# Two transformer layers behind an expert block on one Trainium2 core: the attention's last projection as seven block products

## The chip, the cores and the metric

The kernel runs on one core of one Trainium2 chip. The metric is the device time of one execution in microseconds (us), as the median of several runs. The engines are named by their work: TensorE multiplies matrices (PE in the profile, PEld for its weight loads), VectorE is DVE, ScalarE is ACT, GpSimd is POOL, and SyncE (SP) issues the transfers. Everything is in 32-bit floats.

## The reference, cut to what matters

There are 256 tokens of 1024 features. A first block (a hybrid mixer and 32 routed experts) is followed by two equal layers. Only the end of a layer's attention part is touched:

```python
for l in range(DEPTH_2):                       # 2 layers
    ...                                        # two attentions give y_a, y_b (256 x 512)
    merged = gate_a * (y_a @ w_proj_a[l]) + gate_b * (y_b @ w_proj_b[l])   # 256 x 1024
    x = x + merged @ w_out[l]                  # w_out 1024 x 1024: the product changed here
    h = rms_norm_2(x, norm_ffn[l])
    u = causal_dwconv(h @ w_up[l], conv_w[l], conv_b[l])
    val, gat = u[..., :D_FF], u[..., D_FF:]
    x = x + (jax.nn.silu(gat) * val) @ w_down[l]
```

## The kernel before, in words

The five engines run five written-out programs, and semaphores are all that ties them. Each engine takes its instructions in the order in which they were written. There is no planner; the order of work is the order of the text, in `layers_t` (TensorE), `layers_v` (VectorE), `layers_s` (ScalarE), `layers_pool` (GpSimd) and `layers_sync` (SyncE).

**Tiles.** Tokens lie in two tiles of 128 (`tt`), features in eight tiles of 128 (`KT` = 8), and output columns in two halves of 512 (`CH`). One accumulator bank holds 128 x 512 floats; the eight banks are dealt out in turn by `layer_plan`. TensorE waits for `room` in a bank, fills it and raises `full`; the engine that empties it raises `free`, on which `taken` and the next `room` wait. A 32-bit product of one 128 x 128 tile with 128 x 512 appears in the trace as two MATMUL records.

**Weights.** In the layers a ring of four slots (2 MB each) holds the weights. SyncE loads load n into slot n mod 4 as soon as the last reader of load n-4 has raised its flag; `loads2` lists each load with its reader. The two halves of `w_out` are loads 14 and 15, in slots 2 and 3.

**The stretch around the change, by engine.** TensorE: the last values product (L2358), then the second gated projection `pb` in four banks (`project_t`, L2407), then the output projection `wo` (L2416 to L2424): for each token tile and each column half, eight products over the features, 32 in all. Then twelve short bfloat16 products that nobody reads (`keep_running`, L597), and the transposes of the normed `h`, first token tile 0, then tile 1 (`features_by_tile`, L2282); then the up projection (L606).

VectorE: the four banks of the first projection `pa` times their gates (L2056); for each of four `pb` banks a product with the gates (L2060) and the sum of both (L2064), which writes two feature tiles of `mT` and raises `mg`; then `norm_v`: each bank of `wo` is added to its quarter of x as it comes (L1878), and for each token tile ScalarE squares both quarters (L2131), VectorE sums (L1884), GpSimd takes the root (L1823) and VectorE scales x into `h` (L1894). Tile 0 is normed while TensorE still works on tile 1.

**The down projection is already made the other way.** Its inner dimension is taken in 11 pairs of feature tiles. For a pair the left factor is a 2 x 2 block matrix (token tiles by the two feature tiles: a11, a12, a21, a22), and the right factor too (the two feature tiles by column halves: b11 to b22). Seven products replace eight:

```
s1 = a21 + a22   s2 = s1 - a11   s3 = a11 - a21   s4 = a12 - s2
t1 = b12 - b11   t2 = b22 - t1   t3 = b22 - b12   t4 = b21 - t2
dm0 = a11 b11    dn0 = a12 b21   dn1 = s4 b22     dn3 = s1 t1
dm1 = s2 t2      dm2 = s3 t3     dn2 = a22 t4
u = dm0 + dm1    quarter 0 = dm0 + dn0            quarter 1 = u + dn3 + dn1
quarter 2 = u + dm2 + dn2                         quarter 3 = u + dm2 + dn3
```

`act_sums` (L2072 to L2075, four operations of 128 x 128) and `weight_sums` (L2084 to L2087, four of 128 x 512) make the sums on VectorE; `top_sums` and `low_sums` in `norm_v` put the seven banks together (L1843 to L1867). A helper `then(ins)` makes VectorE wait for its own instruction where the next reads what it wrote.

Of the kernel before, what the change touches and what calls it, by code (L numbers as in the profile page):

```python
# [18 lines left out]
ALU = mybir.AluOpType  # L19
# [92 lines left out]
def layer_plan():  # L112
    p = Plan()
    for name, n in (("hT", 4), ("cv", 1), ("qi", 2), ("m1", 2), ("m2", 2), ("kiT", 1), ("ix0", 2), ("ix1", 4),
# [4 lines left out]
                    ("wo", 4), ("fT", 4), ("up", 2 * UPC), ("dm", 3), ("dn", 4)):  # L119
        p.add(name, n)  # L120
    return p
# [109 lines left out]
def split(ap, n):  # L231
    return ap.rearrange("p (a b) -> p a b", a=n)
# [47 lines left out]
    "yconv", "fexp", "act",  # L280
    "a_sum", "w_sum", "pair",
    "out",
# [3 lines left out]
def build_program(nc, A, consts, out):  # L286
# [4 lines left out]
    with ctx:  # L291
# [45 lines left out]
        def area(at, n):  # L337
            return arena[:, at:at + n]
# [1378 lines left out]
        loads2.append((4, D, [cols("w_proj_a_2", 0, D)], ("pa", 3)))  # L1717
        loads2.append((4, D, [cols("w_proj_b_2", 0, D)], ("pb", 3)))
        for i in range(2):
            loads2.append((KT, CH, [cols("w_out_2", i * CH, (i + 1) * CH)], ("wo", 2 + i)))  # L1720
        for i in range(UPC):
# [54 lines left out]
        def layers_sync(sp):  # L1776

            sp.wait_ge(S["acc_f"], 1)
            for l in range(LAYERS):
                BL = layer_banks(l)  # L1780
                for n, (kts, width, srcs, reader) in enumerate(loads2):
# [16 lines left out]
                    if n == RING2 - 1:  # L1798
# [5 lines left out]
                        sp.dma_start(normw[0][:], A["norm_ffn_2"][l].partition_broadcast(P)).then_inc(L["in_ffn"], 16)  # L1804
                    if reader == ("wo", 3):

                        if l < LAYERS - 1:
                            layer_params(sp, l + 1)
# [28 lines left out]

        def norm_v(v, BL, name, event, w, then=None):

            def quarter(j):  # L1840
                return x[:, j // 2, j % 2 * CH:(j % 2 + 1) * CH]

            def top_sums():  # L1843
                u, y = yval[0], yval[1]
                v.wait_ge(*BL.ready("dm", 0))
                then(v.tensor_tensor(quarter(0), quarter(0), BL.bank("dm", 0)[:], ALU.add))
                v.wait_ge(*BL.ready("dm", 1))
                v.tensor_copy(u, BL.bank("dm", 0)[:]).then_inc(BL.free("dm", 0), 1)
                v.wait_ge(*BL.taken("dm", 0))
                v.tensor_tensor(u, u, BL.bank("dm", 1)[:], ALU.add).then_inc(BL.free("dm", 1), 1)  # L1850
                v.wait_ge(*BL.ready("dn", 0))
                v.tensor_tensor(quarter(0), quarter(0), BL.bank("dn", 0)[:], ALU.add).then_inc(BL.free("dn", 0), 1)
                v.wait_ge(*BL.ready("dn", 3))
                v.wait_ge(*BL.taken("dm", 1))
                then(v.tensor_tensor(y, u, BL.bank("dn", 3)[:], ALU.add))
                then(v.tensor_tensor(quarter(1), quarter(1), y, ALU.add))
                v.wait_ge(*BL.ready("dn", 1))
                v.tensor_tensor(quarter(1), quarter(1), BL.bank("dn", 1)[:], ALU.add).then_inc(BL.free("dn", 1), 1)

            def low_sums():  # L1860
                u = yval[0]
                then(v.tensor_tensor(quarter(3), quarter(3), BL.bank("dn", 3)[:], ALU.add))
                v.wait_ge(*BL.ready("dm", 2))
                v.tensor_tensor(u, u, BL.bank("dm", 2)[:], ALU.add).then_inc(BL.free("dm", 2), 1)
                v.wait_ge(*BL.taken("dm", 2))
                then(v.tensor_tensor(quarter(2), quarter(2), u, ALU.add))
                v.tensor_tensor(quarter(3), quarter(3), u, ALU.add).then_inc(BL.free("dn", 3), 1)  # L1867

            for tt in range(TT):
                if name == "dn" and tt == 0:  # L1870
                    top_sums()
                elif name == "dn":
                    v.wait_ge(*BL.ready("dn", 2))
                    v.tensor_tensor(quarter(2), quarter(2), BL.bank("dn", 2)[:], ALU.add).then_inc(BL.free("dn", 2), 1)
                else:
                    for j in (2 * tt, 2 * tt + 1):
                        v.wait_ge(*BL.ready(name, j))
                        v.tensor_tensor(quarter(j), quarter(j), BL.bank(name, j)[:], ALU.add).then_inc(BL.free(name, j), 1)  # L1878
                if event == 2 * LAYERS:
# [4 lines left out]
                v.tensor_scalar(ms[:, tt:tt + 1], sa[:, tt, 0:1], sa[:, tt, 1:2], EPS, ALU.add, ALU.add).then_inc(L["ms"], 1)  # L1884
                if name == "dn" and tt == 0:
                    low_sums()
# [11 lines left out]

        V_LINKS = 109 + 2 * UPC + 2 * UPC + 5

        def layers_v(v):
            for l in range(LAYERS):
# [150 lines left out]
                for j in range(4):  # L2053
                    g = gate_s[:, 2 * j:2 * j + 2, :]
                    v.wait_ge(*BL.ready("pa", j))
                    v.tensor_tensor(g, split(BL.bank("pa", j)[:], 2), g, ALU.mult).then_inc(BL.free("pa", j), 1)  # L2056
                for j in range(4):
                    t = split(mtmp[j % 2], 2)
                    v.wait_ge(*BL.ready("pb", j))
# [7 lines left out]
                def act_sums(p):  # L2067
                    s1, s2, s3, s4 = (a_sums[p][:, i, :] for i in range(4))
                    a11, a21 = (actT[:, 2 * p, tt * P:(tt + 1) * P] for tt in range(TT))
                    a12, a22 = (actT[:, 2 * p + 1, tt * P:(tt + 1) * P] for tt in range(TT))  # L2070
                    v.wait_ge(L["act"], UPC * l + p + 1)
                    then(v.tensor_tensor(s1, a21, a22, ALU.add))  # L2072
                    v.tensor_tensor(s3, a11, a21, ALU.subtract)
                    then(v.tensor_tensor(s2, s1, a11, ALU.subtract))
                    v.tensor_tensor(s4, a12, s2, ALU.subtract).then_inc(L["a_sum"], 1)  # L2075

                def weight_sums(p):
                    t1, t2, t3, t4 = (w_sums[p % HELD][:, i, :] for i in range(4))
                    w, landed, value = w2_slot(NL - DNC + p // 2, l)
                    k = 2 * p % 4  # L2080
                    b11, b12 = w[:, k, 0:CH], w[:, k, CH:D]
                    b21, b22 = w[:, k + 1, 0:CH], w[:, k + 1, CH:D]
                    v.wait_ge(landed, value)
                    then(v.tensor_tensor(t1, b12, b11, ALU.subtract))  # L2084
                    v.tensor_tensor(t3, b22, b12, ALU.subtract)
                    then(v.tensor_tensor(t2, b22, t1, ALU.subtract))
                    v.tensor_tensor(t4, b21, t2, ALU.subtract).then_inc(L["w_sum"], 1)  # L2087

# [160 lines left out]
        def layers_t(pe):  # L2249
            for l in range(LAYERS):  # L2250
# [618 lines left out]
```

## Time and profile before

| | |
|---|---|
| median of 3 runs | 2212.95 us (2206.88 to 2217.66) |
| profiled execution, its own time | 2206.54 us |
| its span in the trace | 2204.5 us |
| granted TensorE clock, mean | 0.993 |
| TensorE busy | 2115.7 us, 96% |
| VectorE busy | 979.7 us, 44% |
| output projection in layer 0 | 1479.7 to 1507.2 us |
| output projection in layer 1 | 1948.5 to 1976.0 us |

The span is the stretch from the first to the last instruction; the execution's own time is 2.04 us longer. In the rows a "bank" is an accumulator, "ring" the weight slots and everything that lies in the two idle ones, "arena", "hbuf" and "hTbuf" are working areas. Idle time in brackets stands ahead of the instruction, with what ended it. The clock that TensorE was granted (PEclk) is given as a share of full speed: 1.00 is 2.4 GHz and 0.50 is 1.2 GHz.

### The profile page before, as it was taken

To read this page: it belongs to the slowest core of one execution; us is meant where nothing else is said; L and a number is where in the kernel's file an instruction comes from. 1 tells how busy PE (TensorE), PEld (TensorE's weight loads), DVE (VectorE), ACT (ScalarE), POOL (GpSimd) and SP (SyncE) were. 2 spreads that over 40 slices of the span, in tenths; PEclk is the share of its full clock that TensorE was granted. 3 is DMA by queue.
4 is the path that set the end of the run, shared out by engine and by line. 5 is a ranking of instruction groups with operands and counts; after the bars stand their busy time and mean duration, and the time that the engine had idled before them with its cause. 6 is when DMAs were issued, how large, how long until landed. Compare 5 with 4: busy or idle time off the path is not lost.

```text
span 2204.5 us, 24055 instructions
## 1 busy us (share of the span) xinstructions
PE 2115.7 (96%) x9704; PEld 1164.4 (53%) x9704; DVE 979.7 (44%) x1561; ACT 333.7 (15%) x737; POOL 48.3 (2%) x30
## 2 busy tenths in 40 slices
PE   6998999999999999999999899999999999999999
PEld 4855743333333333333333365886885557868874
DVE  1555535333323333223332226843676256725684
ACT  1123110000000000000000112321110113311110
POOL 0000200000000000000000002000000011000000
PEclk9988999999999999999999999999999999999999
DMA  9556079999998999999999754343443534243441
GB/s 371 209 222 266 18 249 402 428 428 429 428 425 325 428 429 428 428 428 429 428 429 428 284 192 172 115 135 124 151 151 129 179 117 168 100 153 120 153 162 63
DMA packets 132001, 590.91 MB, mean 268 GB/s; under 512 B 9142, under 2 KB 65638, under 8 KB 104026
## 3 DMA queue, kind: packets, MB, share of 16 engines
q1 hardware_dynamic: 131930, 589.90, 67.6%
q8 instruction: 53, 0.87, 0.2%
q14 instruction: 18, 0.15, 0.0%
HBM read 588.81 MB, written 3.16 MB: 269 GB/s over the span
## 4 chain that ended last, share of the span: by engine, by line
PE 70%; DMA 21%; DVE 5%; ACT 2%; issue 1%; POOL 1%; SPq 0%; POOLq 0%; DVEq 0%
PE bank L606 21%; DMA ring<-in_w_dram 20%; PE bank L1415 18%; PE bank L616 8%; PE bank L2444 6%; PE bank L2407 3%; PE bank L819 2%; PE bank L2422 2%; PE bank L1469 1%; PE bank L1396 1%; PE bank L2787 1%; DMA ring<-in_w_ada_dram 1%; PE bank L543 1%; PE bank L1428 1%; PE bank L2358 1%
## 5 line engine op out<-in xcount | busy, mean ns | idle before, releaser
L1415 PE MATMUL bank<-ring,arena 128*64 128x512 f32 x3168 | 702.7, 595 | 28.3 <-DMA ring<-in_w_dram 27.6
L606 PE MATMUL bank<-hTbuf,ring 128*128 128x256 f32 x2368 | 515.9, 380 | 2.8 <-ACT hTbuf L2676 2.6
L606 PEld LDWEIGHTS bank<-hTbuf,ring 128*128 128x128 f32 x2368 | 450.1, 190 | 67.1 <-issue 5.9
L1415 PEld LDWEIGHTS bank<-ring,arena 128*64 128x64 f32 x3168 | 219.6, 137 | 500.5 <-issue 428.8
L1117 DVE TENSOR_SCALAR arena<-bank 128x512 f32<-128x512 f32 x33 | 22.8, 692 | 395.9 <-PE bank L1415 395.9
L616 PE MATMUL bank<-ring,hTbuf 128*128 128x512 f32 (+2 forms) x384 | 151.2, 554 | 0.0
L2097 DVE SCALAR_TENSOR_TENSOR arena<-bank,arena 128x254 f32<-128x254 f32 (+1 forms) x176 | 76.6, 477 | 84.4 <-ACT arena L2241 82.8
L616 PEld LDWEIGHTS bank<-ring,hTbuf 128*128 128x128 f32 x384 | 72.6, 190 | 75.1 <-issue 71.8
L1121 DVE RECIPROCAL arena<-arena 128x512 f32<-128x512 f32 x33 | 110.6, 3353 | 1.1
L1242 ACT ACTIVATE arena<-arena 128x512 f32<-128x512 f32 x33 | 20.8, 629 | 535.0 <-DVE arena L1117 535.0
L1141 DVE TENSOR_TENSOR arena<-bank,arena 128x512 f32<-128x512 f32 x33 | 22.8, 692 | 128.4 <-PE bank L1415 128.4
L2241 ACT ACTIVATE arena<-bank,arena 128x256 f32<-128x256 f32 x88 | 44.9, 561 | 209.4 <-PE bank L606 209.4
L2109 DVE RECIPROCAL arena<-arena 128x512 f32<-128x512 f32 x22 | 73.8, 3353 | 0.8
L1469 PE MATMUL bank<-arena 64*128 64x512 f32 x264 | 65.6, 615 | 8.0 <-DVE arena L1141 8.0
L1396 PE MATMUL bank<-hbuf,arena 128*64 128x512 f32 x256 | 62.0, 605 | 0.0
L2407 PE MATMUL bank<-arena,ring 128*128 128x256 f32 (+1 forms) x320 | 56.8, 339 | 0.0
L2422 PE MATMUL bank<-ring 128*128 128x512 f32 x128 | 55.3, 592 | 0.0
L1238 ACT ACTIVATE arena<-bank 128x512 f32<-128x512 f32 x33 | 19.7, 597 | 228.4 <-PE bank L1403 228.4
L2407 PEld LDWEIGHTS bank<-arena,ring 128*128 128x128 f32 x320 | 50.4, 191 | 5.4 <-issue 0.7
L2023 DVE RECIPROCAL arena<-arena 128x1024 f32<-128x1024 f32 x8 | 52.4, 6553 | 0.3
L1137 DVE COPY arena<-bank 128x256 f32<-128x256 f32 x33 | 14.0, 424 | 73.6 <-PE bank L1409 73.6
L2444 PE MATMUL bank<-arena 128*128 128x512 f32 x96 | 44.1, 592 | 0.0
(462 smaller groups left out, 1849.0 us busy)
## 6 DMA issues: line engine op xcount, KB each, us to landing
ring<-in_w_dram SPq DMA_DIRECT2D x192, 2048.0 KB, 22.6
ring<-in_w_up_dram SPq DMA_DIRECT2D x44, 1024.0 KB, 7.0
ring<-in_w_in_dram SPq DMA_DIRECT2D x21, 2048.0 KB, 8.6
ring<-in_w_ada_dram SPq DMA_DIRECT2D x12, 2048.0 KB, 8.6
ring<-in_w_down_dram SPq DMA_DIRECT2D x10, 2048.0 KB, 7.8
ring<-in_w_out_dram SPq DMA_DIRECT2D x6, 2048.0 KB, 8.0
ring<-in_w_in_dram SPq DMA_DIRECT2D x4, 1024.0 KB, 13.8
ring<-in_w_proj_a_dram SPq DMA_DIRECT2D x2, 2048.0 KB, 8.3
```

Source lines behind the costliest of these rows:

```text
L606: ins = pe.matmul(B.bank(name, j)[:, i * T:(i + 1) * T], w[:, k, (first + i) * P:(first + i + 1) * P], hT[:, k, :], start=(k == 0), stop=( ...
L616: ins = pe.matmul(B.bank(name, j)[:, 0:width], xs(k), ws(k), start=(k == 0), stop=(k == kts - 1))
L1121: v.reciprocal(eb, eb).then_inc(F["s1"], 1)
L1396: ins = pe.matmul(XB[g * SLOTS:(g + 1) * SLOTS, :], psel[:, tt, :], h[:, tt, g * CH:(g + 1) * CH], start=(tt == 0), stop=(tt == 1))
L1415: ins = pe.matmul(bank[g * SLOTS:(g + 1) * SLOTS, :], lhsT, rhs[:, g * CH:(g + 1) * CH], start=start, stop=stop)
L1469: pe.matmul(ACC[2 * tt + g][:], pgt[par][64 * g:64 * g + 64, tt, :], ysb[64 * g:64 * g + 64, :], start=False, stop=False, skip_group_check ...
L2023: v.reciprocal(gs, gs).then_inc(L["gsig"], 1)
L2097: ins = v.scalar_tensor_tensor(out=y2[:, k, back:], in0=pb[:, k, 0:T - back], scalar=conv_cols[:, 44 * (2 - back) + m:44 * (2 - back) + m ...
L2109: then(v.reciprocal(fe[i % 2], fe[i % 2]))
L2407: ins = pe.matmul(BL.bank(name, j)[:, i * T + c0:i * T + c1], w[:, k, (2 * j + i) * P:(2 * j + i + 1) * P], src[:, k, c0:c1], start=(k == ...
L2422: ins = pe.matmul(BL.bank("wo", 2 * tt + half)[:], mT[:, k, tt * P:(tt + 1) * P], ws[half][:, k, :], start=(k == 0), stop=(k == KT - 1))
L2444: return pe.matmul(bank[:], lhsT, rhs, start=(p == 0), stop=(p == NPR - 1))
```

## The change

The output projection is made by the same seven products, with four pairs of feature tiles (p = 0 to 3). Three more banks (`wm`) are dealt out ahead of `wo`, which moves all later banks by three. VectorE makes the sums of the weights (`out_sums`: waits until both halves of `w_out` have landed, then four operations of 128 x 512) and of the gated sums (`mix_sum`, four of 128 x 128). Pairs 0 and 1 of `out_sums` stand ahead of the loop over the `pb` banks, pairs 2 and 3 inside it, ahead of the evacuation of bank 2 and of bank 3. `norm_v` now treats `wo` as it treated `dn`. Both halves of `w_out` name `wm` bank 1 as the reader that frees their slots. The four helpers `left_sums`, `right_sums`, `act_sums` and `weight_sums` do what the old text of the last two did.

```diff
-                    ("wo", 4), ("fT", 4), ("up", 2 * UPC), ("dm", 3), ("dn", 4)):
+                    ("wm", 3), ("wo", 4), ("fT", 4), ("up", 2 * UPC), ("dm", 3), ("dn", 4)):
...
+        mix_sums = [split(area(at, 4 * P), 4) for at in (6 * D, 6 * D + 4 * P, 8 * D, 8 * D + 4 * P)]
+        wo_sums = [split(buf, 4) for buf in (area(4 * D, 4 * CH), hTbuf[:], extra(2 * D, 4 * CH), area(11776, 4 * CH))]
...
-            loads2.append((KT, CH, [cols("w_out_2", i * CH, (i + 1) * CH)], ("wo", 2 + i)))
+            loads2.append((KT, CH, [cols("w_out_2", i * CH, (i + 1) * CH)], ("wm", 1)))
...
+            more = {"dn": "dm", "wo": "wm"}.get(name)
...
             for tt in range(TT):
-                if name == "dn" and tt == 0:
+                if tt == 0:
                     top_sums()
-                elif name == "dn":
-                    v.wait_ge(*BL.ready("dn", 2))
-                    v.tensor_tensor(quarter(2), quarter(2), BL.bank("dn", 2)[:], ALU.add).then_inc(BL.free("dn", 2), 1)
                 else:
-                    for j in (2 * tt, 2 * tt + 1):
-                        v.wait_ge(*BL.ready(name, j))
-                        v.tensor_tensor(quarter(j), quarter(j), BL.bank(name, j)[:], ALU.add).then_inc(BL.free(name, j), 1)
+                    v.wait_ge(*BL.ready(name, 2))
+                    v.tensor_tensor(quarter(2), quarter(2), BL.bank(name, 2)[:], ALU.add).then_inc(BL.free(name, 2), 1)
...
+                def mix_sum(p):
+                    v.wait_ge(L["mg"], 4 * l + p + 1)
+                    left_sums(mT, p, mix_sums[p], L["mix_sum"])
+
+                def out_sums(p):
+                    halves = [w2_slot(N_WO + half, l) for half in range(2)]
+                    for w, landed, value in halves:
+                        v.wait_ge(landed, value)
+                    (b11, b12), (b21, b22) = ([w[:, 2 * p + k, :] for w, landed, value in halves] for k in range(2))
+                    right_sums(b11, b12, b21, b22, wo_sums[p], L["wo_sum"])
+
+                out_sums(0)
+                out_sums(1)
                 for j in range(4):
+                    if j >= 2:
+                        out_sums(j)
                     t = split(mtmp[j % 2], 2)
                     v.wait_ge(*BL.ready("pb", j))
...
                     v.tensor_tensor(mT[:, 2 * j:2 * j + 2, :], gate_s[:, 2 * j:2 * j + 2, :], t, ALU.add).then_inc(L["mg"], 1)
-                norm_v(v, BL, "wo", 2 * l + 1, normw[0])
+                    mix_sum(j)
+                norm_v(v, BL, "wo", 2 * l + 1, normw[0], then)
...
-                for tt in range(TT):
-                    for half in range(2):
-                        pe.wait_ge(*BL.room("wo", 2 * tt + half))
-                        for k in range(KT):
-                            if tt == 0 and half == 0 and k % 2 == 0:
-                                pe.wait_ge(L["mg"], 4 * l + k // 2 + 1)
-                            ins = pe.matmul(BL.bank("wo", 2 * tt + half)[:], mT[:, k, tt * P:(tt + 1) * P], ws[half][:, k, :],
-                                            start=(k == 0), stop=(k == KT - 1))
-                        ins.then_inc(BL.full("wo", 2 * tt + half), 1)
+                for name, n in (("wm", 3), ("wo", 4)):
+                    for j in range(n):
+                        pe.wait_ge(*BL.room(name, j))
+
+                def out_product(name, j, lhs, rhs):
+                    for p in range(4):
+                        ins = pe.matmul(BL.bank(name, j)[:], lhs(p), rhs(p), start=(p == 0), stop=(p == 3))
+                    ins.then_inc(BL.full(name, j), 1)
+
+                for p in range(4):
+                    pe.wait_ge(L["mg"], 4 * l + p + 1)
+                    ins = pe.matmul(BL.bank("wm", 0)[:], mT[:, 2 * p, 0:P], ws[0][:, 2 * p, :], start=(p == 0), stop=(p == 3))
+                ins.then_inc(BL.full("wm", 0), 1)
+                out_product("wo", 0, lambda p: mT[:, 2 * p + 1, 0:P], lambda p: ws[0][:, 2 * p + 1, :])
+                pe.wait_ge(L["mix_sum"], 4 * l + 4)
+                out_product("wo", 1, lambda p: mix_sums[p][:, 3, :], lambda p: ws[1][:, 2 * p + 1, :])
+                pe.wait_ge(L["wo_sum"], 4 * l + 4)
+                out_product("wo", 3, lambda p: mix_sums[p][:, 0, :], lambda p: wo_sums[p][:, 0, :])
+                out_product("wm", 1, lambda p: mix_sums[p][:, 1, :], lambda p: wo_sums[p][:, 1, :])
+                out_product("wm", 2, lambda p: mix_sums[p][:, 2, :], lambda p: wo_sums[p][:, 2, :])
+                out_product("wo", 2, lambda p: mT[:, 2 * p + 1, P:T], lambda p: wo_sums[p][:, 3, :])
```

## Rows read from the trace of the kernel before

**Rows 1.** The page's table of engines: busy time, share of the span, instructions.
```profile
PE 2115.7 (96%) x9704; PEld 1164.4 (53%) x9704; DVE 979.7 (44%) x1561; ACT 333.7 (15%) x737; POOL 48.3 (2%) x30
```
**Rows 2.** The page's chain of waits that ended last, by engine.
```profile
PE 70%; DMA 21%; DVE 5%; ACT 2%; issue 1%; POOL 1%; SPq 0%; POOLq 0%; DVEq 0%
```
**Rows 3.** TensorE's timeline, layer 0: start, duration, engine, line, operation, count, idle before.
```profile
1465.65 14.20 PE L2407 MATMUL bank<-arena,ring 128*128 128x128 f32 x80
...
1479.69 27.63 PE L2422 MATMUL bank<-ring 128*128 128x512 f32 x64
1507.16 2.75 PE L597 MATMUL bank<-con 128*128 128x512 bf16 x12
1509.75 1.04 PE L2282 MATMUL bank<-con,hbuf 128*128 128x128 f32 x8
1511.19 1.09 PE L2282 MATMUL bank<-con,hbuf 128*128 128x128 f32 x8 [0.40 <-DVE hbuf L1894]
```
**Rows 4.** VectorE's timeline of the same stretch.
```profile
1461.70 0.69 DVE L2056 TENSOR_TENSOR arena<-bank,arena 128x512 f32<-128x512 f32 x1 [2.02 <-PE bank L2407]
1469.53 0.69 DVE L2060 TENSOR_TENSOR arena<-bank,arena 128x512 f32<-128x512 f32 x1 [7.14 <-PE bank L2407]
1470.25 0.69 DVE L2064 TENSOR_TENSOR ring<-arena 128x512 f32<-128x512 f32 x1
1472.98 0.69 DVE L2060 TENSOR_TENSOR arena<-bank,arena 128x512 f32<-128x512 f32 x1 [2.04 <-PE bank L2407]
...
1480.62 0.69 DVE L2064 TENSOR_TENSOR ring<-arena 128x512 f32<-128x512 f32 x1
...
1507.36 0.69 DVE L1878 TENSOR_TENSOR x<-x,bank 128x512 f32<-128x512 f32 x1 [6.18 <-PE bank L2422]
```
**Rows 5.** VectorE's timeline in layer 0's down projection: its sums.
```profile
1673.43 0.29 DVE L2072 TENSOR_TENSOR arena<-ring 128x128 f32<-128x128 f32 x1
...
1674.50 0.68 DVE L2084 TENSOR_TENSOR hTbuf<-ring 128x512 f32<-128x512 f32 x1
...
1677.15 0.68 DVE L2084 TENSOR_TENSOR arena<-ring 128x512 f32<-128x512 f32 x1
```
**Rows 6.** SyncE's timeline: the issue of both halves of w_out in layer 0.
```profile
1418.07 19.16 SPq L1796 DMA_DIRECT2D ring<-in_w_out_dram  x2
```
**Rows 7.** The page's DMA issues: count, KB each, median us to landing.
```profile
ring<-in_w_out_dram SPq DMA_DIRECT2D x6, 2048.0 KB, 8.0
```
**Rows 8.** VectorE's timeline behind layer 0's down projection (norm_v with dn).
```profile
1719.03 0.69 DVE L1848 COPY arena<-bank 128x512 f32<-128x512 f32 x1 [1.88 <-PE bank L2444]
...
1726.76 0.69 DVE L1858 TENSOR_TENSOR x<-x,bank 128x512 f32<-128x512 f32 x1 [1.23 <-PE bank L2444]
...
1728.36 0.68 DVE L1862 TENSOR_TENSOR x<-x,bank 128x512 f32<-128x512 f32 x1
...
1730.78 0.69 DVE L1867 TENSOR_TENSOR x<-x,arena 128x512 f32<-128x512 f32 x1
1731.39 1.41 DVE L1894 SCALAR_TENSOR_TENSOR hbuf<-x,small,normw 128x512 f32<-128x512 f32 x2
1732.71 0.68 DVE L1874 TENSOR_TENSOR x<-x,bank 128x512 f32<-128x512 f32 x1
```
**Rows 9.** TensorE's timeline behind layer 0's down projection.
```profile
1731.63 2.75 PE L597 MATMUL bank<-con 128*128 128x512 bf16 x12
...
1737.13 1.09 PE L2282 MATMUL bank<-con,hbuf 128*128 128x128 f32 x8 [1.87 <-DVE hbuf L1894]
```
**Rows 10.** TensorE's timeline in the first block: two of its idle stretches.
```profile
34.84 7.44 PE L606 MATMUL bank<-hTbuf,ring 128*128 128x256 f32 x26 [2.58 <-ACT hTbuf L2676]
...
210.33 2.05 PE L819 MATMUL bank<-hbuf,arena 128*128 128x128 f32 x16 [3.21 <-DVE arena L717]
```
**Rows 11.** Stretches of 1 us: busy time of each engine, granted clock, DMA share, GB/s.
```profile
35.00:36.00 1.00, 1.00 (x3) 0.82 (x4) 0.00 (x0) 0.00 (x0) 0.00 (x0) 0.50 1.01 424
...
211.00:212.00 1.00, 1.00 (x12) 1.00 (x10) 0.00 (x0) 0.47 (x1) 0.00 (x0) 1.00 1.15 492
```

More of the change, by code:

```diff
@@ L280 @@
     "yconv", "fexp", "act",
-    "a_sum", "w_sum", "pair",
+    "a_sum", "w_sum", "pair", "mix_sum", "wo_sum",
     "out",
@@ L1718, in build_program @@
         loads2.append((4, D, [cols("w_proj_b_2", 0, D)], ("pb", 3)))
+        N_WO = len(loads2)
         for i in range(2):
-            loads2.append((KT, CH, [cols("w_out_2", i * CH, (i + 1) * CH)], ("wo", 2 + i)))
+            loads2.append((KT, CH, [cols("w_out_2", i * CH, (i + 1) * CH)], ("wm", 1)))
         for i in range(UPC):
@@ L1804, in layers_sync @@
                         sp.dma_start(normw[0][:], A["norm_ffn_2"][l].partition_broadcast(P)).then_inc(L["in_ffn"], 16)
-                    if reader == ("wo", 3):
+                    if n == N_WO + 1:
                         if l < LAYERS - 1:
@@ L1836, in layers_pool, with norm_v @@
                 roots_p(pool, 2 * l + 1)
-        def norm_v(v, BL, name, event, w, then=None):
+        def norm_v(v, BL, name, event, w, then):
             def quarter(j):
                 return x[:, j // 2, j % 2 * CH:(j % 2 + 1) * CH]
+            more = {"dn": "dm", "wo": "wm"}.get(name)
             def top_sums():
                 u, y = yval[0], yval[1]
[L1845 to L1855, printed above, removed]
+                v.wait_ge(*BL.ready(more, 0))
+                then(v.tensor_tensor(quarter(0), quarter(0), BL.bank(more, 0)[:], ALU.add))
+                v.wait_ge(*BL.ready(more, 1))
+                v.tensor_copy(u, BL.bank(more, 0)[:]).then_inc(BL.free(more, 0), 1)
+                v.wait_ge(*BL.taken(more, 0))
+                v.tensor_tensor(u, u, BL.bank(more, 1)[:], ALU.add).then_inc(BL.free(more, 1), 1)
+                v.wait_ge(*BL.ready(name, 0))
+                v.tensor_tensor(quarter(0), quarter(0), BL.bank(name, 0)[:], ALU.add).then_inc(BL.free(name, 0), 1)
+                v.wait_ge(*BL.ready(name, 3))
+                v.wait_ge(*BL.taken(more, 1))
+                then(v.tensor_tensor(y, u, BL.bank(name, 3)[:], ALU.add))
@@ L1856, in top_sums @@
                 then(v.tensor_tensor(quarter(1), quarter(1), y, ALU.add))
-                v.wait_ge(*BL.ready("dn", 1))
-                v.tensor_tensor(quarter(1), quarter(1), BL.bank("dn", 1)[:], ALU.add).then_inc(BL.free("dn", 1), 1)
+                v.wait_ge(*BL.ready(name, 1))
+                v.tensor_tensor(quarter(1), quarter(1), BL.bank(name, 1)[:], ALU.add).then_inc(BL.free(name, 1), 1)
             def low_sums():
                 u = yval[0]
-                then(v.tensor_tensor(quarter(3), quarter(3), BL.bank("dn", 3)[:], ALU.add))
@@ L1863, in low_sums @@
-                v.wait_ge(*BL.ready("dm", 2))
-                v.tensor_tensor(u, u, BL.bank("dm", 2)[:], ALU.add).then_inc(BL.free("dm", 2), 1)
-                v.wait_ge(*BL.taken("dm", 2))
+                then(v.tensor_tensor(quarter(3), quarter(3), BL.bank(name, 3)[:], ALU.add))
+                v.wait_ge(*BL.ready(more, 2))
+                v.tensor_tensor(u, u, BL.bank(more, 2)[:], ALU.add).then_inc(BL.free(more, 2), 1)
+                v.wait_ge(*BL.taken(more, 2))
                 then(v.tensor_tensor(quarter(2), quarter(2), u, ALU.add))
-                v.tensor_tensor(quarter(3), quarter(3), u, ALU.add).then_inc(BL.free("dn", 3), 1)
+                v.tensor_tensor(quarter(3), quarter(3), u, ALU.add).then_inc(BL.free(name, 3), 1)
@@ L1884, in norm_v @@
                 v.tensor_scalar(ms[:, tt:tt + 1], sa[:, tt, 0:1], sa[:, tt, 1:2], EPS, ALU.add, ALU.add).then_inc(L["ms"], 1)
-                if name == "dn" and tt == 0:
+                if tt == 0:
                     low_sums()
@@ L1897, in norm_v @@
                 ins.then_inc(L["h_new"], 1)
-        V_LINKS = 109 + 2 * UPC + 2 * UPC + 5
+        V_LINKS = 109 + 4 * UPC + 16 + 10
         def layers_v(v):
@@ L2056, in layers_v, with left_sums, right_sums, act_sums @@
                     v.tensor_tensor(g, split(BL.bank("pa", j)[:], 2), g, ALU.mult).then_inc(BL.free("pa", j), 1)
+                def left_sums(src, p, out, flag):
+                    s1, s2, s3, s4 = (out[:, i, :] for i in range(4))
+                    a11, a21 = (src[:, 2 * p, tt * P:(tt + 1) * P] for tt in range(TT))
+                    a12, a22 = (src[:, 2 * p + 1, tt * P:(tt + 1) * P] for tt in range(TT))
+                    then(v.tensor_tensor(s1, a21, a22, ALU.add))
+                    v.tensor_tensor(s3, a11, a21, ALU.subtract)
+                    then(v.tensor_tensor(s2, s1, a11, ALU.subtract))
+                    v.tensor_tensor(s4, a12, s2, ALU.subtract).then_inc(flag, 1)
+                def right_sums(b11, b12, b21, b22, out, flag):
+                    t1, t2, t3, t4 = (out[:, i, :] for i in range(4))
+                    then(v.tensor_tensor(t1, b12, b11, ALU.subtract))
+                    v.tensor_tensor(t3, b22, b12, ALU.subtract)
+                    then(v.tensor_tensor(t2, b22, t1, ALU.subtract))
+                    v.tensor_tensor(t4, b21, t2, ALU.subtract).then_inc(flag, 1)
+                def act_sums(p):
+                    v.wait_ge(L["act"], UPC * l + p + 1)
+                    left_sums(actT, p, a_sums[p], L["a_sum"])
+                def weight_sums(p):
+                    w, landed, value = w2_slot(NL - DNC + p // 2, l)
+                    k = 2 * p % 4
+                    v.wait_ge(landed, value)
+                    right_sums(w[:, k, 0:CH], w[:, k, CH:D], w[:, k + 1, 0:CH], w[:, k + 1, CH:D], w_sums[p % HELD], L["w_sum"])
+                def mix_sum(p):
[4 more added lines that the diff above has]
+                    for w, landed, value in halves:
+                        v.wait_ge(landed, value)
+                    (b11, b12), (b21, b22) = ([w[:, 2 * p + k, :] for w, landed, value in halves] for k in range(2))
+                    right_sums(b11, b12, b21, b22, wo_sums[p], L["wo_sum"])
+                out_sums(0)
+                out_sums(1)
                 for j in range(4):
+                    if j >= 2:
+                        out_sums(j)
                     t = split(mtmp[j % 2], 2)
@@ L2064, in layers_v @@
                     v.tensor_tensor(mT[:, 2 * j:2 * j + 2, :], gate_s[:, 2 * j:2 * j + 2, :], t, ALU.add).then_inc(L["mg"], 1)
-                norm_v(v, BL, "wo", 2 * l + 1, normw[0])
[L2067 to L2087, printed above, removed]
+                    mix_sum(j)
+                norm_v(v, BL, "wo", 2 * l + 1, normw[0], then)
                 for i in range(UPC):
```

## The prediction

> **What bounds the kernel now.** I read the table of engines first: TensorE is busy for 96% of the span and VectorE for 44% [rows 1]. Then the chain of waits: TensorE holds 70% of it and transfers 21% [rows 2]; by its lines the transfers belong to the expert weights of the first block, far from this change. So inside the layers the order of TensorE's work is the time, and the timelines of one stretch decide. TensorE goes from the second gated projection (ends 1479.69) into the output projection without a gap, and out of it at 1507.16 into the filler products [rows 3]. Behind it stands a tail that no product hides: the last bank is added at 1507.36, and the transposes of token tile 1 start at 1511.19 [rows 3, 4], 4.03 us after the last product. Layer 1 shows the same distances. VectorE, meanwhile, waits: 7.14 us before bank 0 of the second projection and about 2 us before each later one [rows 4]. These gaps are where the new sums have to fit.
>
> **The change part by part.** I call E the moment at which TensorE starts the fillers, 1507.16 before.
>
> *Four products fewer.* 64 records take 27.47 us (1507.16 - 1479.69), so one of the 32 products takes 0.858 us. Four fewer save 3.43 us a layer. All of it is on the path.
>
> *Sums on VectorE.* A set of four 128 x 512 sums takes 2.65 us (1677.15 - 1674.50), one of 128 x 128 takes 1.07 us (1674.50 - 1673.43) [rows 5]; there are 22 of each in the trace, from the same places, so I take these figures as they are. The weights are there: w_out's second half is issued at 1436.9 and lands about 8.0 us later [rows 6, 7], long before 1462. Their wait thus ends at once.
>
> VectorE's order, with bank j's product 0.72 us ahead of the sum [rows 4]:
> - It leaves `pa` at 1462.39 (rows 4: 1461.70 + 0.69). Two weight sets end at 1467.7, inside the 7.14 us gap; hidden, with 1.8 us to spare.
> - Bank 0 at 1469.53: product, sum, `mix_sum`: 0.72 + 0.72 + 1.07 = 2.51 us, within the 3.45 us (1472.98 - 1469.53) between banks. Bank 1 at 1472.98, done at 1475.49.
> - Weight set 2: to 1478.14. Bank 2, ready since 1476.4, is only now read; with its mix sum to 1480.65.
> - Weight set 3: to 1483.30. Bank 3: the sum starts at 1484.02 and ends at 1484.71; before, it ended at 1481.31 (1480.62 + 0.69) [rows 4].
>
> *The wait that this makes.* The first new product (a11 b11) asks for `mg` once for each pair. TensorE starts it at 1479.69, and three pairs take it to 1482.27. The fourth needs the sum that ends at 1484.71: a stall of about 2.5 us, with all of TensorE's remaining work queued behind it. Before, the same sum was needed only behind six products (5.15 us), at 1484.8, and cost nothing. Left are 1 + 24 = 25 products: 1484.77 + 25 x 0.858 = 1506.23. So E comes 0.93 us earlier instead of 3.43. The later waits are met: the mix sums end at 1485.8 and are needed at 1489.1, the weight sums end at 1483.3 and are needed at 1492.5. The wait for seven banks at once rests on bank 2 of `pb`, emptied at 1478.83, 0.9 us ahead of 1479.69; it is free, but would cost what VectorE slips beyond that.
>
> *The tail.* VectorE may not touch `wm` bank 1 before it is full, at E - 6.87 (eight products follow), and stops there with everything that it could do already (`wo` 0, 1, 3) queued behind. From a filled bank to VectorE's start are 0.20 us [rows 3, 4]. So the copy starts at E - 6.67. A step that reads the result before it costs 0.72 (rows 4), one that doesn't 0.61 (1731.39 - 1730.78) [rows 8]. Copy, u, quarter 0, y, quarter 1, quarter 1: 0.72 + 0.61 + 0.61 + 0.72 + 0.72 brings the last one to a start at E - 3.29. From there to the first of the low sums 1.60 (1728.36 - 1726.76), three more low sums at 0.72, then 0.61 to the norm of tile 0, 1.32 to quarter 2 (1732.71 - 1731.39), and 4.42 through square, root and norm to the transposes of tile 1 (1737.13 - 1732.71) [rows 8, 9]: E + 6.82. Before it was E + 4.03. The tail grows by 2.79 us. The chain never waits for TensorE after its start, since `wm` 2 is full at E - 3.43 and `wo` 2 at E, 2.4 us before it is read. What is late here is VectorE, which has nine operations between the fifth product and the norm of tile 0 where it had one bank to add. Bounds: nothing (the tail stays 4.03), and 0.72 for every step, which gives E + 7.05 and +3.0. I take 2.79, since the down projection shows just these operations.
>
> *Hidden or nil.* The wait of two w_up loads moves from `wo` 2 and 3 to `wm` 1 (up to 7 us earlier); they serve the third and fourth group of up products, ahead of which TensorE has the fillers, the transposes and two whole groups, so 0 either way. Banks move by three: the tail of a layer finds `wm` 2 (for the transposes) freed at E - 0.3 against a use after E + 2.6, and the next layer's first transposes find `dn` 2 freed at 1733.4 against 1734.2, where the fillers end (1731.63 + 2.59, the distance of rows 3) [rows 8, 9]. I take 0; each would cost what it slips. The up projection and the down projection are untouched.
>
> **Sum.** A layer: -3.43 + 2.50 + 2.79 = +1.86 us; two layers +3.7 us. The span becomes 2208.2, the profiled execution 2206.54 + 3.7 = 2210.2. The median of the runs lies 6.4 us above that execution; carried over: 2212.95 + 3.7 = 2216.7 us.
>
> **A rule that speaks against the change.** In the new order TensorE idles in two places a layer: 2.5 us in the first product, and 3.2 us between the transposes of tile 0 (end E + 3.6) and tile 1. The trace shows both outcomes for such stretches: behind 2.58 us of idle the clock was 0.50, that is 1.2 GHz, and behind 3.21 us it was 1.00, 2.4 GHz [rows 10, 11]. The Trainium skill, page "TensorE: Matmul & The Clock Gate", Part 1, says that the full clock is not the resting state: idling between bursts sends it to the lower level, and work has to bring it back. The trace agrees in part, as these two rows differ.
>
> **The rivals.**
> 1. *The clock falls in some of the new gaps.* For it: the 2.58 us gap. Against it: the 3.21 us gap, and dense products on both sides of the first gap. The price: the row of 0.50 is the first of three whole microseconds like it behind the 2.58 us gap, so some 3.2 us from 34.84 on ran at half speed [rows 10, 11], which costs 1.6 us. One to four falls: +1.6 to +6.4, so +5.3 to +10.1 in all; in the middle 2212.95 + 7 = 2220 us.
> 2. *The first stall is not there* (VectorE gets through the loop in time, or the third and fourth set cost less among waits): -3.43 + 2.79 = -0.64 a layer, 2211.7 us. Against it: two sets (5.3 us) stand ahead of the last `mg`, where 3 us of gaps are left.
> 3. *The saving lands*, the other side: VectorE's work disappears in the gaps at both ends, the tail stays 4.03, and four products a layer are gone: 2 x -3.43 = -6.9, 2206.1 us. It decides itself at `wm` 1: only if VectorE had its nine operations done by E would it hold. For it: VectorE is idle for most of the stretch. Against it: the order of the products, which fills `wm` 1 fifth of seven.
> 4. *VectorE slips past 0.9 us*, so that `room` holds back the whole projection, or the shifted banks hold the transposes: +1 us a layer on top, +5.7, 2218.7 us.
>
> **How the numbers follow.** Forecast 0.45, rival 1 0.30, rival 2 0.08, rival 3 0.07, rival 4 0.10. The largest and the smallest of these cases differ by 17 us, and the three runs of before by 10.8 us. 0.5%, or 11 us, is about what a measurement can tell from no change. Range: from 2207 (rival 3, and the forecast with a low draw of the runs) to 2226 (rival 1 with a high one). Faster by over 0.5% needs a gain of over 11 us, more than even rival 3 has: 0.03. Slower needs nearly all four falls, or a smaller number of them and a high median: 0.10. Within: 0.87.
>
> **What would show each step.** In the profile after: 56 records a layer for the output projection at an unchanged 592 ns; a gap of about 2.5 us in it, put down to VectorE's sum into `mT`, 2.6 us behind its start; VectorE going through its operations of the loop without idle time from bank 2 on; the fillers starting about 0.9 us earlier, measured from the end of the second projection; the transposes of tile 1 behind 3.2 us of idle time; the clock in both gaps. The forecast is wrong if the first gap is missing or the tail stays near 4 us, and if the later products show over 592 ns.

## The result, and the profile after

| | before | after |
|---|---|---|
| median of 9 runs each | 2213.13 us (2206.88 to 2217.66) | 2222.68 us (2220.02 to 2225.33) |
| profiled execution's span | 2204.5 us | 2218.5 us |
| granted TensorE clock, mean | 0.993 | 0.988 |

The ratio is 1.0043, with a 95% interval of 1.0031 to 1.0055: 9.5 us slower, 6.9 to 12.2. The time lies in the range of the prediction, 6.0 us above its point. The change removes 8 products of 0.858 us and makes the kernel slower. Of the 14.0 us between the two spans, 3.4 lie ahead of the change (VectorE's first product on a `pb` bank starts at 1472.94 us in place of 1469.53); from there to the end of the span the kernel after is 10.6 us longer.

The page's table of engines and the chain by engine, of the kernel after (compare [rows 1, 2]):

```profile
PE 2119.2 (96%) x9688; PEld 1167.4 (53%) x9688; DVE 1018.6 (46%) x1641; ACT 333.3 (15%) x737; POOL 48.3 (2%) x30
...
PE 67%; DMA 22%; DVE 6%; ACT 2%; issue 1%; POOL 1%; SPq 0%; POOLq 0%; DVEq 0%
```

TensorE has 16 records fewer and is busy 3.5 us longer: work of the same kind has become slower, in part ahead of the change. VectorE has 38.9 us more, of which the chain shows only one percent. TensorE's timeline of layer 0 (start, duration, engine, line, operation, count, idle before; compare [rows 3]) says where:

```profile
1469.07 14.20 PE L2428 MATMUL bank<-arena,ring 128*128 128x128 f32 x80
1483.10 2.74 PE L2448 MATMUL bank<-ring 128*128 128x512 f32 x6
1488.18 1.90 PE L2448 MATMUL bank<-ring 128*128 128x512 f32 x2 [2.34 <-DVE ring L2106]
1489.87 4.57 PE L2443 MATMUL bank<-ring 128*128 128x512 f32 x8
1494.28 3.60 PE L2443 MATMUL bank<-ring,arena 128*128 128x512 f32 x8
...
1511.44 2.75 PE L597 MATMUL bank<-con 128*128 128x512 bf16 x12
1514.15 1.06 PE L2303 MATMUL bank<-con,hbuf 128*128 128x128 f32 x8
1518.35 1.27 PE L2303 MATMUL bank<-con,hbuf 128*128 128x128 f32 x8 [3.13 <-DVE hbuf L1895]
```

The first product stops for 2.34 us before its last pair. Six records take 2.57 us from start to start at the pace of [rows 3], so the seventh comes 2.51 us late (1488.18 instead of 1485.67). Behind the stop 8 records of 128 x 512 take 4.57 us, where the next 8 take 3.60. And the transposes of token tile 1 come behind 3.13 us of idle time, where 0.40 stood [rows 3]. VectorE's timeline of the same stretch (compare [rows 4, 8]):

```profile
1478.91 0.68 DVE L2069 TENSOR_TENSOR ring<-ring 128x512 f32<-128x512 f32 x1
...
1481.56 0.68 DVE L2102 TENSOR_TENSOR arena<-bank,arena 128x512 f32<-128x512 f32 x1
...
1484.07 0.68 DVE L2069 TENSOR_TENSOR arena<-ring 128x512 f32<-128x512 f32 x1
...
1486.72 0.68 DVE L2102 TENSOR_TENSOR arena<-bank,arena 128x512 f32<-128x512 f32 x1
1487.44 0.69 DVE L2106 TENSOR_TENSOR ring<-arena 128x512 f32<-128x512 f32 x1
...
1504.85 0.69 DVE L1853 COPY arena<-bank 128x512 f32<-128x512 f32 x1 [14.04 <-PE bank L2443]
```

From weight set 2 (1478.91) to the last sum into mT (1487.44) VectorE has no idle time. TensorE resumes at 1488.18, as that sum ends. Then VectorE waits 14.04 us for `wm` 1, with the banks of `wo` 0, 1 and 3 full before it. Last, the clock in stretches of 1 us behind the gaps of both layers (the number before the last two):

```profile
1489.00:1490.00 1.00, 1.00 (x3) 0.46 (x2) 0.29 (x1) 0.00 (x0) 0.00 (x0) 0.50 1.10 353
1521.00:1522.00 1.00, 1.00 (x4) 0.82 (x3) 0.00 (x0) 0.00 (x0) 0.00 (x0) 0.50 0.00 0
1963.00:1964.00 1.00, 1.00 (x2) 0.34 (x1) 0.56 (x3) 0.00 (x0) 0.00 (x0) 0.50 1.10 348
1995.00:1996.00 1.00, 1.00 (x4) 0.81 (x3) 0.00 (x0) 0.00 (x0) 0.00 (x0) 0.50 0.00 0
```

TensorE ran at 1.2 GHz behind each of the four gaps.

I measure a layer's stretch from VectorE's first product on a `pb` bank to ScalarE's first reading of an `up` bank, since what lies between those two is all that the change touches. It falls into three parts at E (the first filler) and at the transposes of tile 1. All figures are us, from the starts of such rows of each profiled execution; where the layers differ, both are given.

| kernel | first `pb` product to E | E to transposes of tile 1 | from there to ScalarE's first `up` read | total | against before, two layers |
|---|---|---|---|---|---|
| before | 37.63 | 4.03 | 8.40 | 50.06 | |
| after | 38.50 | 6.91 | 9.86 / 10.08 | 55.27 / 55.48 | +10.6 |
| late sums (e1) | 34.41 | 6.69 | 9.36 / 9.47 | 50.46 / 50.57 | +0.9 |
| fillers (e2) | 37.04 | 6.69 | 8.40 | 52.13 | +4.1 |
| no sums (e3) | 34.41 | 6.70 | 10.95 / 11.00 | 52.06 / 52.11 | +4.0 |
| sums only (e4) | 37.90 | 3.81 | 8.40 | 50.11 | +0.1 |
| early adds (e5) | 38.50 | 4.65 | 8.40 | 51.55 | +3.0 |
| late sums, early adds (e6) | 34.20 | 4.64 | 8.40 | 47.24 | -5.7 |
| the same, squares turned (e7) | 34.20 | 4.03 | 8.40 | 46.63 | -6.9 |
| late sums, `wm` 1 fourth (e8) | 34.20 | 4.91 | 8.40 | 47.51 | -5.1 |

(The profiles of e1 to e4 show 11 of the twelve fillers, and their first starts 0.2 us later against the last product than elsewhere. So E is read 0.2 us late there: the first part is 0.2 us shorter than the table has it and the second as much longer. In e1 they are 34.2 and 6.9.)

The rest of each profile can be set beside this. From the first `pb` product of layer 0 to the end of the span it is, against before (734.97 us): after +10.6, e1 +2.5, e2 +4.2, e3 +4.2, e4 +0.1, e5 +3.0, e6 -5.6, e7 -7.5, e8 -3.5 us. Where that differs from the last column by more than 0.2 us, a cause is given below (e1, e7, e8). Ahead of that product, where nothing was changed, the ten profiles differ by up to 10.2 us (1469.53 in before, 1479.74 in e5). Much of this is the clock in the first 300 us: one minus the granted clock, added up over stretches of 1 us, gives 15.4 us in before and 25.6 us in e5. Most of the spread between runs of one kernel can thus come from a part that the change does not touch.

### The profile page after: what moved, and what is told of

Same layout as the page of the kernel before. It is cut to its first block, busy times and chain, and to the rows that moved or that the text cites. A ratio compares the mean times of both kernels' runs of the same rounds, so it can differ in the third digit from the quotient of the medians.

```text
span 2218.5 us, 24125 instructions
## 1 busy us (share of the span) xinstructions
PE 2119.2 (96%) x9688; PEld 1167.4 (53%) x9688; DVE 1018.6 (46%) x1641; ACT 333.3 (15%) x737; POOL 48.3 (2%) x30
## 4 chain that ended last, share of the span: by engine, by line
PE 67%; DMA 22%; DVE 6%; ACT 2%; issue 1%; POOL 1%; SPq 0%; POOLq 0%; DVEq 0%
DMA ring<-in_w_dram 21%; PE bank L606 21%; PE bank L1415 17%; PE bank L616 8%; PE bank L2477 6%; PE bank L819 2%; PE bank L2428 2%; PE bank L2443 1%; PE bank L2820 1%; PE bank L1469 1%; PE bank L1396 1%; DMA ring<-in_w_ada_dram 1%; PE bank L543 1%; PE bank L1428 1%; PE bank L2379 1%
## 5 line engine op out<-in xcount | busy, mean ns | idle before, releaser
L2477 PE MATMUL bank<-ring 128*128 128x512 f32 x88 | 41.2, 594 | 1.8 <-DVE arena L2118 1.8
```

The costliest lines, as they stand in the source:

```text
L2477: return pe.matmul(bank[:], lhsT, rhs, start=(p == 0), stop=(p == NPR - 1))
```

## The experiments

My theory after the result: a layer gains 3.43 us by four products, and pays a stall (2.34 us idle), a longer tail (2.9), and 1.2 GHz behind both gaps (1.8 and 1.5), 5.1 us net; with the stall from start to start, 2.51, it is 5.3, beside 5.21 and 5.41 in the stretches. The main rival: VectorE's extra work costs time of its own, by slowing TensorE or wherever it stands. e1 to e4 are set beside one group of 35 runs of the kernel before (2213.5 us), e5 to e8 beside another of 19 (2213.97 us).

**e1: weight sets 2 and 3 behind the loop.**

```diff
                 for j in range(4):
-                    if j >= 2:
-                        out_sums(j)
                     t = split(mtmp[j % 2], 2)
...
                     mix_sum(j)
+                out_sums(2)
+                out_sums(3)
                 norm_v(v, BL, "wo", 2 * l + 1, normw[0], then)
```

> Weight sets 2 and 3 stand behind the loop over the second projection's banks. My theory (waits and clock): the stall of 2.34 us in the first product goes, and with it the half-speed stretch behind it (1.80 us); the sets still end before TensorE asks for them. The output projection then takes 28 x 0.858 = 24.0 us, the tail stays at 6.9 us with its own half-speed stretch (1.46 us). A layer gains 4.1 us on the changed kernel, 8.3 in all: about 2214.4 us, within 1.5 us of the kernel before. Rival (VectorE's sums slow TensorE's reads, or take their time wherever they stand): no more than the 2.34 us a layer or nothing comes back, 2218 to 2222 us.

Measured: 2217.48 us beside 2213.5; ratio 1.001 (0.9994 to 1.0026). TensorE's timeline, layer 0:

```profile
1489.53 3.60 PE L2448 MATMUL bank<-ring 128*128 128x512 f32 x8
1492.96 3.60 PE L2443 MATMUL bank<-ring 128*128 128x512 f32 x8
...
1520.47 1.97 PE L2303 MATMUL bank<-con,hbuf 128*128 128x128 f32 x8 [3.14 <-DVE hbuf L1895]
```

The stall is gone and the first product takes 3.43 us; the first part of the stretch is 4.09 us shorter than after, 4.3 with the filler that is missing (4.1 expected). The transposes behind the gap that is left last 1.97 us instead of 1.09, at a granted clock of 0.50. The median is 3 us over the 2214.4 of the expectation, which the interval (-1.3 to +5.8 us) still holds; the stretches, +0.9 us, agree with it. The profile has 1.6 us more between the two stretches (420.36 us in place of 418.76), all of it behind the 1.87 us gap in the down projection's tail. That gap did no harm in before [rows 9] or after; here the clock fell behind it, as it did in e8:

```profile
1747.38 1.09 PE L2303 MATMUL bank<-con,hbuf 128*128 128x128 f32 x8 [1.87 <-DVE hbuf L1895]
...
1749.00:1750.00 1.00, 1.00 (x3) 0.82 (x4) 0.00 (x0) 1.00 (x4) 0.00 (x0) 0.50 1.05 378
```

**e2: the changed kernel with fillers in both gaps.** Ten stand ahead of the first product's last pair, twelve between the transposes of tile 0 and of tile 1.

```diff
+                    if p == 3:
+                        keep_running(pe, BL.bank("wo", 0), 10)
                     pe.wait_ge(L["mg"], 4 * l + p + 1)
...
                     for tt in range(TT):
+                        if name == "fT" and tt == 1:
+                            pe.wait_ge(*BL.room("up", 0))
+                            keep_running(pe, BL.bank("up", 0), 12)
```

> The changed kernel with 10 filler products (bfloat16, read by nobody) ahead of the fourth product and 12 between the transposes of token tile 0 and 1; every wait stays. Theory: both gaps and the tail stay as long as they are, but the clock is 1.00 behind both, which gives back 1.80 + 1.46 us a layer, 6.5 in all: about 2216.2 us. Rival (the longer times behind the gaps are refill of TensorE's queue or the transfer of w_up running at the same time, not the clock): the same products stay slow, 2222.7 us.

Measured: 2216.36 us beside 2213.5; ratio 1.0015 (1.0002 to 1.0028), so 6.3 us under the changed kernel, 6.5 expected. TensorE's timeline of layer 0, then the clock behind both gaps:

```profile
1483.30 2.10 PE L597 MATMUL bank<-con 128*128 128x512 bf16 x9
1485.61 1.12 PE L2453 MATMUL bank<-ring 128*128 128x512 f32 x2 [0.20 <-DVE ring L2106]
1486.57 3.60 PE L2446 MATMUL bank<-ring 128*128 128x512 f32 x8
```

```profile
1486.00:1487.00 1.00, 1.00 (x3) 0.38 (x2) 0.93 (x4) 0.00 (x0) 0.00 (x0) 1.00 1.09 359
...
1516.00:1517.00 1.00, 1.00 (x6) 0.87 (x5) 0.00 (x0) 0.62 (x2) 0.00 (x0) 1.00 0.00 0
```

No wait is shorter: TensorE still resumes on VectorE's sum, and the tail is as long. Yet the 8 records behind it take 3.60 us in place of 4.57, at a clock of 1.00, while the w_up transfer runs beside them just as in the changed kernel (DMA share 1.09 here, 1.10 there). So the transfer is not what slowed them. The Trainium skill, page "TensorE: Matmul & The Clock Gate", section "Why this matters for your kernels", advises against idle gaps between bursts of products; the trace agrees in these two places, with 0.50 behind four gaps, and 1.00 once fillers stand in them.

**e3: seven products without any sums.** The products read raw tiles of mT and w_out, and all 32 sums a layer are left out, so the output is another. Both halves of `w_out` name `wo` 2 as their last reader in place of `wm` 1, so the slots come free later.

```diff
-                out_sums(0)
-                out_sums(1)
...
-                    mix_sum(j)
...
-                out_product("wm", 1, lambda p: mix_sums[p][:, 1, :], lambda p: wo_sums[p][:, 1, :])
+                out_product("wm", 1, lambda p: mT[:, 2 * p + 1, 0:P], lambda p: ws[0][:, 2 * p, :])
```

> Seven products, but on the raw tiles of mT and w_out: all sums of VectorE (32 instructions a layer) are left out, so the output is not the reference's. Theory: no stall and no slow clock in the projection (24.0 us), the tail of norm_v unchanged at 6.9 us with its half-speed stretch: as with the late sums, about 2214.4 us. This tells whether sums placed late are really free. If VectorE's sums cost something of their own (rival), this kernel is faster than the one with late sums by what they cost.

Measured: 2216.6 us beside 2213.5; ratio 1.001 (0.9995 to 1.0026). Up to the transposes it equals e1 to 0.01 us (34.41 and 6.70): the 16 weight sums and 16 mix sums a layer, where they stand in e1, cost nothing. In one point I was wrong: the same gap of 3.15 us cost 2.6 us of low clock here (10.95 - 8.40), 1.0 in e1 and 1.5 to 1.7 in the changed kernel. The price of a fall is no constant. The clock stood below 1.00 for longer: in layer 0 from 1517 to 1524 us in e3, from 1519 to 1524 in e1. No run shows the missing sums to be the reason; why it stayed low longer is open.

**e4: all the sums, and eight products.** The projection and its adds are those of before; VectorE makes the sums where the change has them, and nobody reads them. Against the kernel before:

```diff
+                out_sums(0)
+                out_sums(1)
                 for j in range(4):
+                    if j >= 2:
+                        out_sums(j)
...
+                    mix_sum(j)
```

> The kernel before, eight block products and the old adds, with all the sums of the change put into VectorE's program where the change has them; nobody reads them. Theory: the last sum into mT comes at the same late moment, but TensorE asks for it only behind six products, so nothing moves: within 0.5 us a layer of before, 2213 to 2214 us. Rival (VectorE's load itself slows TensorE): 2 to 5 us a layer slower, 2217 to 2223 us.

Measured: 2213.47 us beside 2213.5; ratio 0.9999 (0.9987 to 1.0011). VectorE's last sum into mT starts 14.52 us behind its first `pb` product (1491.25 - 1476.73), as late as after (1487.44 - 1472.94), and the projection is not held:

```profile
1486.89 27.68 PE L2447 MATMUL bank<-ring 128*128 128x512 f32 x64
```

No idle time stands ahead of it, and 64 records take 27.68 us, 0.05 more than in [rows 3]. VectorE's sums alone cost nothing (-2.9 to +2.4 us by the ratio, +0.1 in the stretches): the main rival falls. The stall is made by the order of TensorE's requests together with the late sums.

**e5: early adds.** The changed kernel, but VectorE adds each bank as it comes: for `wo`, `early_sums` stands in for `top_sums`, and `low_sums` leaves out the add of `wo` 3 that is now made early. The first lines of the new function are left out here.

```diff
+            def early_sums():
+                ...
+                v.wait_ge(*BL.ready("wo", 0))
+                v.tensor_tensor(quarter(0), quarter(0), BL.bank("wo", 0)[:], ALU.add).then_inc(BL.free("wo", 0), 1)
+                v.wait_ge(*BL.ready("wo", 1))
+                then(v.tensor_tensor(quarter(1), quarter(1), BL.bank("wo", 1)[:], ALU.add))
+                v.wait_ge(*BL.ready("wo", 3))
+                then(v.tensor_tensor(quarter(1), quarter(1), BL.bank("wo", 3)[:], ALU.add))
+                then(v.tensor_tensor(quarter(3), quarter(3), BL.bank("wo", 3)[:], ALU.add))
+                v.wait_ge(*BL.taken("wm", 0))
+                v.wait_ge(*BL.ready("wm", 1))
+                v.tensor_tensor(u, u, BL.bank("wm", 1)[:], ALU.add).then_inc(BL.free("wm", 1), 1)
+                v.wait_ge(*BL.taken("wm", 1))
+                v.tensor_tensor(quarter(1), quarter(1), u, ALU.add).then_inc(BL.free("wo", 1), 1)
```

> The changed kernel, where VectorE adds wm 0, wo 0, wo 1 and wo 3 as soon as each is full, and keeps only u and the last sum of quarter 1 for behind wm 1. Theory: the norm of tile 0 no longer waits for six operations behind the fifth product; the tail is set by the last product and is 4.6 us (0.2 + 4.42) in place of 6.9, TensorE idles about 1 us in it instead of 3.1, so the clock stays at 1.00 there. The first stall (2.34 us) and its slow stretch (1.8 us) stay. A layer against before: -3.43 + 2.34 + 1.80 + 0.6 = +1.3; 2216.1 us beside 2213.5. Rival (the tail is set by the chain of square, root and norm whatever VectorE does before it): the tail stays at 6.9 us and the time at 2222 us.

Measured: 2214.43 us beside 2213.97; ratio 1.0003 (0.9989 to 1.0016). TensorE's timeline, layer 0:

```profile
1518.24 2.75 PE L597 MATMUL bank<-con 128*128 128x512 bf16 x12
1520.84 1.04 PE L2325 MATMUL bank<-con,hbuf 128*128 128x128 f32 x8
1522.89 1.09 PE L2325 MATMUL bank<-con,hbuf 128*128 128x128 f32 x8 [1.01 <-DVE hbuf L1917]
```

The tail is 4.65 us (4.6 expected), the gap in it 1.01 us, and the clock holds there: the third part is 8.40 again. Its first part, 38.50, is that of the changed kernel.

**e6: late sums and early adds.** The edits of e1 and e5 in one kernel:

```diff
-                    if j >= 2:
-                        out_sums(j)
...
+                out_sums(2)
+                out_sums(3)
...
-                    top_sums()
+                    if name == "wo":
+                        early_sums()
+                    else:
+                        top_sums()
```

> Both edits together: weight sets 2 and 3 behind the loop, and the early adds. Theory: no stall, no slow clock, tail 4.6 us: a layer -3.43 + 0.6 = -2.8 against before, -5.7 in all: 2207.8 us beside 2213.5. Rival (a saving in this stretch is given back elsewhere, as the late sums alone measured some us over before): 2212 us or more.

Measured: 2206.01 us beside 2213.97; ratio 0.997 (0.9959 to 0.9982), 6.6 us faster than before by the ratio (4.0 to 9.1), 5.7 in the stretches. With stall and tail both mended, the saving lands.

**e7: and the squares turned.** On top of e6, ScalarE squares the right half of tile 1 first, in both norms.

```diff
                     for tt in range(TT):
-                        for half in range(2):
+                        for half in ((0, 1), (1, 0))[tt]:
```

> As the one before, and ScalarE squares the right half of token tile 1 first, which is complete earlier, so that only one square follows the last add (for dn as well). Theory: 0.6 us off the tail, which is then 4.0 us as in the kernel before; the whole saving of four products a layer lands: -6.9 - 0.6 (the down projection's tail of layer 0) = -7.5: about 2206 us. Rival (the tail's length is set by TensorE's fillers and the transposes of tile 0): no difference to the version without it, 2207.8 us.

Measured: 2203.97 us beside 2213.97; ratio 0.9949 (0.9934 to 0.9964), the fastest. TensorE's timeline and then VectorE's, layer 0:

```profile
1510.12 2.75 PE L597 MATMUL bank<-con 128*128 128x512 bf16 x12
...
1514.15 1.09 PE L2325 MATMUL bank<-con,hbuf 128*128 128x128 f32 x8 [0.40 <-DVE hbuf L1917]
```

```profile
1503.55 0.69 DVE L1879 TENSOR_TENSOR arena<-arena,bank 128x512 f32<-128x512 f32 x1 [2.05 <-PE bank L2465]
1504.27 0.69 DVE L1881 TENSOR_TENSOR x<-x,arena 128x512 f32<-128x512 f32 x1
...
1510.32 0.69 DVE L1901 TENSOR_TENSOR x<-x,bank 128x512 f32<-128x512 f32 x1
```

Two operations stand behind `wm` 1 where six stood, and the last add starts 0.20 us behind E: the last product sets the tail again, 4.03 us as in [rows 3]. The stretches give -6.9 us and the down projection's tail -0.6 (4.89 against 5.50): -7.5. The ratio says -11.3 (-14.6 to -8.0). The profile has -7.5 from the first `pb` product to the end, so these two account for all that the trace shows behind that point. The 4 us between lie ahead of the change or in the spread of six runs, and why they are there stays open.

**e8: `wm` 1 fourth.** Late sums and the old adds, but TensorE makes `wm` 1 ahead of `wo` 3.

```diff
+                out_product("wm", 1, lambda p: mix_sums[p][:, 1, :], lambda p: wo_sums[p][:, 1, :])
                 out_product("wo", 3, lambda p: mix_sums[p][:, 0, :], lambda p: wo_sums[p][:, 0, :])
-                out_product("wm", 1, lambda p: mix_sums[p][:, 1, :], lambda p: wo_sums[p][:, 1, :])
```

> Weight sets 2 and 3 behind the loop, VectorE's adds as in the change, but TensorE makes wm 1 fourth and wo 3 fifth. Theory (the tail is long because wm 1 comes fifth of seven): VectorE has the copy, u and quarter 0 done before wo 3 is full, and the tail shrinks from 6.9 to 4.9 us; a layer -3.43 + 0.85 against before, 2208.3 us. Rival (the tail depends on the number of VectorE's operations, not on when wm 1 is full): it stays at 6.7 us as with the late sums alone, 2215 to 2217 us.

Measured: 2207.4 us beside 2213.97; ratio 0.9968 (0.9955 to 0.998). The tail is 4.91 us (4.9 expected) with the same number of VectorE's operations: what counts is when `wm` 1 is full. The profile has 1.7 us more between the stretches, behind the 1.88 us gap in the down projection's tail, as in e1.

## Why the prediction was right and wrong, step by step

- **Four products fewer, -3.43 us a layer.** Right: e6 and e7 show 37.63 - 34.20 = 3.43.
- **The stall in the first product, 2.5 us.** Right in place, cause (released by the sum into mT) and size: 2.34 us idle, 2.51 from start to start. e1 removes it by moving two sets, e4 shows that the late sum alone does not make it.
- **E 0.93 us earlier.** Wrong: 0.87 later (38.50 against 37.63). The missing 1.80 us are the half-speed stretch behind the stall, which the sum of the likeliest case had at nothing. e2 gives back 1.46 of them, about 1.7 when the filler that is missing from its profile is counted.
- **The tail, 4.03 to 6.82.** Right: 6.91. The cause, six operations behind the fifth product, is shown twice: by moving four of them ahead of it (e5), and by moving the product (e8).
- **Hidden or nil: transfers, shifted banks, the wait for seven banks.** No wait of theirs appears; e6 and e7 have the same banks and transfers and lose nothing.
- **The clock.** This is the step that failed. The forecast put 0.45 on a clock that holds, and 0.30 on rival 1 (one to four falls, +5.3 to +10.1 in all). All four gaps fell, and the time is +9.5, near that rival's end. I had weighed one row where 3.21 us of idle time did no harm against one where 2.58 did [rows 10, 11]. In the runs here all ten gaps of 2.3 us or more that stand in these places without fillers (after 4, e1 2, e3 2, e5 2) were followed by slow products. And the row that spoke against rival 1 was one outcome of two. The same 3.21 us gap stands in all ten profiles, and its clock fell in six; the kernel after is one of them:

```profile
210.36 2.48 PE L819 MATMUL bank<-hbuf,arena 128*128 128x128 f32 x16 [3.21 <-DVE arena L717]
...
212.00:213.00 1.00, 1.00 (x6) 1.00 (x6) 0.00 (x0) 0.28 (x2) 0.00 (x0) 0.50 0.99 426
```

  Read from the kernel after, the same place would have spoken for rival 1. The price put on one fall, 1.6 us, was about the mean of what came (1.0 to 2.6).
- **The sum.** Forecast per layer +1.86, measured in the stretches +5.21 and +5.41. Of the difference 3.26 to 3.47 is the clock (1.80 behind the stall, 1.46 to 1.67 behind the tail's gap).
- **Rival 3** (the saving lands: 2206.1) was right on its condition: it asked for VectorE's operations to be done by E. e7 meets that (the last of them ends at 1509.02, E is 1510.12), and its two stretches are 6.9 us shorter, the size that rival 3 gave. That its median, 2203.97, lies near 2206.1 is in part luck: 0.6 us come from the down projection, and 4 are not explained.

## What to carry to other kernels

Where an engine's idle time is to take new work, set the time at which each piece is asked for beside the time at which it ends, in the order of the queue: the same eight weight sums cost 2.3 us of stall a layer ahead of two evacuations, and nothing behind them. Adds of a block scheme should be made as each bank comes, so that the last product and not the first combination sets the tail. A gap of about 2 us or more on TensorE should be priced with its clock: here the clock took 3.3 us a layer on top of 5.2 us of stall and tail, and short fillers in the gap gave it back without touching a wait. The price should be put as a chance, since one profile shows only one outcome of a gap: read the same gap in several profiles first. And where a program is the same up to some instruction, profiles are compared from that instruction on: here this took out up to 10.2 us.

## What the runs showed of the hardware that I had not expected

A gap of 2.34 us with dense products on both sides sufficed to bring TensorE to 1.2 GHz, in both layers of both kernels that had it (after and e5). The same gap can have either outcome in different executions. The 3.21 us gap of [rows 10] was followed or accompanied by 0.50 in six of ten profiles, and the 1.87 to 1.88 us gap in the down projection's tail in two of nine (e1 and e8; e7 has 1.26 us there). The gaps of 1.01 us (e5 and e6) and 1.29 us (e8) were not followed by slow products. The price of a gap of 3.13 to 3.15 us was 1.0 (e1), 1.5 and 1.7 (the two layers of after) and 2.6 us (e3).
